# Value products and output projection laid into the heads of two attentions, with rotary keys padded to full height

## What is computed

```python
def mla_mixer(h, ...):
    proj = h @ w_in                                  # c_q 384, c_kv 256, k_pe 64
    q = rms_norm(c_q, q_a_norm) @ w_uq               # 8 heads x (128 + 64)
    kv = rms_norm(c_kv, kv_a_norm) @ w_ukv           # 8 heads x (128 keys + 128 values)
    q_pe, k_pe = rope(rms_norm(...)), rope(rms_norm(...))
    logits = (q_nope @ k_nope.T + q_pe @ k_pe.T) * scale     # causal
    return (softmax(logits) @ v) @ w_o

def moba_mixer(h, w_qkv, ...):                       # 256 tokens: one block, own keys only
    q, k, v = split(h @ w_qkv)
    logits = rms_norm(q) @ rms_norm(k).T * scale + rel_bias  # causal
    return (softmax(logits) @ v) @ w_o
```

## Time and profile before

| | us |
|---|---|
| median of 3 timed runs | 1106.78 |
| lowest and highest of them | 1105.79, 1111.33 |
| the profiled execution | 1100.91 |
| its span, first to last instruction | 1099.3 |
| TensorE busy | 1036.1 (94%) |
| VectorE busy | 703.4 (64%) |
| ScalarE busy | 529.1 (48%) |
| POOL busy | 99.2 (9%) |

### The profile page before, as it was taken

How to read it: one execution, slowest core, us unless ns; L and a number is a source line. 1 busy time by engine, 2 the same in 40 slices (tenths; PEclk the granted TensorE clock), 3 DMA queues, 4 the chain that set the end, 5 groups by cost and what they waited for, 6 DMA issues and landing times.

```text
span 1099.3 us, 15596 instructions
## 1 busy us (share of the span) xinstructions
PE 1036.1 (94%) x6112; PEld 886.9 (81%) x6112; DVE 703.4 (64%) x946; ACT 529.1 (48%) x712; POOL 99.2 (9%) x77
## 2 busy tenths in 40 slices
PE   7989899999999997989999999999999889999996
PEld 5556789888997875889999887988966678999995
DVE  5645556888736556557676754456477477777774
ACT  2463447766444557444554543553344255445442
POOL 0120004665000010000000000000000000000000
PEclk9997999999999999999999999999999999999998
DMA  8034466767643551547777542334100145445531
GB/s 351 1 126 104 153 232 251 274 241 272 255 158 115 191 191 44 219 159 269 280 281 283 198 184 78 115 118 151 39 1 1 43 175 200 176 172 186 200 148 57
DMA packets 29725, 183.89 MB, mean 167 GB/s; under 512 B 3440, under 2 KB 6128, under 8 KB 10096
## 3 DMA queue, kind: packets, MB, share of 16 engines
q1 hardware_dynamic: 25216, 156.84, 39.2%
q0 software_dynamic: 3456, 25.17, 6.5%
q10 hardware_dynamic: 1008, 1.27, 0.3%
HBM read 180.64 MB, written 2.62 MB: 167 GB/s over the span
## 4 chain that ended last, share of the span: by engine, by line
PE 74%; DVE 13%; ACT 6%; issue 3%; DMA 2%; POOL 1%; ACTq 0%; DVEq 0%; SPq 0%
PE bank L662 20%; PE bank L663 19%; PE bank L664 19%; DVE split L1795 4%; ACT split L1297 4%; PE bank L857 3%; PE bank L671 2%; DMA consts<-in_consts 2%; PE bank L1162 2%; PE bank L1143 1%; PE bank L945 1%; POOL stat L593 1%; PE bank L804 1%; DMA raw<-w_mlp 1%; ACT arena L1298 1%
## 5 line engine op out<-in xcount | busy, mean ns | idle before, releaser
L1795 DVE TENSOR_TENSOR split<-raw,split 128x2048 fp32r<-128x2048 f32 (+1 forms) x123 | 283.7, 2307 | 240.1 <-ACT split L1297 234.5
L1297 ACT ACTIVATE split<-raw 128x2048 fp32r<-128x2048 f32 (+1 forms) x123 | 233.6, 1899 | 267.7 <-PE bank L664 244.9
L662 PE MATMUL bank<-acts,split 128*128 128x256 f32 (+1 forms) x1024 | 290.6, 284 | 2.7 <-DVE acts L1833 1.4
L663 PE MATMUL bank<-acts,split 128*128 128x256 f32 (+1 forms) x1024 | 289.6, 283 | 0.0
L664 PE MATMUL bank<-acts,split 128*128 128x256 f32 (+1 forms) x1024 | 289.6, 283 | 0.0
L662 PE MATMUL bank<-split,acts 128*128 128x512 f32 (+1 forms) x544 | 214.4, 394 | 15.4 <-DVE split L1795 8.3
L663 PE MATMUL bank<-split,acts 128*128 128x512 f32 (+1 forms) x544 | 210.4, 387 | 0.0
L664 PE MATMUL bank<-split,acts 128*128 128x512 f32 (+1 forms) x544 | 210.3, 386 | 0.0
L662 PEld LDWEIGHTS bank<-acts,split 128*128 128x128 f32 (+1 forms) x1024 | 194.7, 190 | 6.2 <-issue 3.3
L663 PEld LDWEIGHTS bank<-acts,split 128*128 128x128 f32 (+1 forms) x1024 | 194.7, 190 | 2.3
L664 PEld LDWEIGHTS bank<-acts,split 128*128 128x128 f32 (+1 forms) x1024 | 194.7, 190 | 0.4
(11 more groups left out here) (245 smaller groups left out, 1189.6 us busy)
## 6 DMA issues: line engine op xcount, KB each, us to landing
raw<-w_mlp SPq DMA_DIRECT2D x64, 1024.0 KB, 4.9
raw<-w_glu SPq DMA_DIRECT2D x22, 1024.0 KB, 5.3
work<-w_ada POOLq DMA_DIRECT2D x12, 1024.0 KB, 5.1
raw<-w_qkv SPq DMA_DIRECT2D x12, 1024.0 KB, 4.8
bias<-w_ada POOLq DMA_DIRECT2D x12, 1024.0 KB, 5.1
arena<-w_glu_down SPq DMA_DIRECT2D x22, 512.0 KB, 3.3
raw<-w_mla_o SPq DMA_DIRECT2D x4, 1024.0 KB, 5.7
raw<-w_moba_o SPq DMA_DIRECT2D x4, 1024.0 KB, 4.8
```

Source lines behind the costliest of these rows:

```text
L662: pe.matmul(out_, a[0], b[0], start=first, stop=False)
L663: pe.matmul(out_, a[0], b[1], start=False, stop=False)
L1297: return act.activation(out_, in_, ACT.Copy)
L1795: v.tensor_tensor(split[:, c % 2, 1, 0:n], raw[:, c % 2, 0:n], split[:, c % 2, 0, 0:n].bitcast(F32), ALU.subtract).then_inc(lo_ready, 1)
```

## The change

1. **Rotary keys.** `kpT` becomes two tiles of full height: one holds the key in partitions 0 to 63 and zeros above, the other zeros below and the key in partitions 64 to 127. POOL writes the zeros after its third root. All four score matmuls of a head are now 128 partitions high.
2. **Value units, attention 0.** Of the four value units, unit 4 follows the rotary query transposes, unit 5 the key transposes, unit 6 stands after S2, unit 7 after O0. ScalarE empties them at matching places, the last two behind exponentials 0 and 1.
3. **Splits of mla_o.** The high part of chunk 0 is made by VectorE. The high part of chunk 1 is made by ScalarE in iteration 5 of the attention, its low part by VectorE in iteration 6; both came after the attention before.
4. **Value chunks, attention 1.** The loop covers only queries and keys, with a mean and a root for each. Queries are scaled and transposed first, then value chunks 0 and 1 are multiplied, keys transposed, then half of chunk 2; the other half stands after S2, the halves of chunk 3 after O0 and O1. The splits of chunks move with them.
5. **Projection.** Chunk 0 of either output projection is issued in two halves (by token tile), after O5 and after O6.
6. **Window attention.** Segment products of a step stand directly behind P(i).

```diff
@@ grid_order
         steps.append(("P", i))
+        steps.extend(x for x in SEGMENTS if SEGMENT_STEP.get(x) == i)
         if i + 3 < 2 * H:
             steps.append(("S", i + 3))
...
-        steps.extend(x for x in SEGMENTS if SEGMENT_STEP.get(x) == i)
@@ program
-        kpT = view(arena, 12288, T)
+        kpT = view(arena, 12288, T), view(arena, 12800, T)
@@ POOL
-            roots(0, 7)
+            roots(0, 3)
+            pool.wait_ge(roots_ready, 3)
+            pool.memset(kpT[0][64:128], 0.0).then_inc(kpe_zeros, 1)
+            pool.wait_ge(kpe_zeros, 1)
+            pool.memset(kpT[1][0:64], 0.0).then_inc(kpe_zeros, 1)
+            pool.wait_ge(kpe_zeros, 2)
+            roots(3, 7)
@@ TensorE
+            def out_products(name, g, t):
+                c, u = GC[name] + g, GU[name] + t
+                if t == 0:
+                    weights_in(c)
...
+            def first_out(name, attention, t):
+                for h in range(4):
+                    small_gone(pe, SU[attention] + unit_c[("O", h)])
+                out_products(name, 0, t)
...
+                    beside(kind, h)
...
-            ukv_products(1)
             pe.wait_ge(heads_normed, 3)
...
+            pe.wait_ge(front_w[7], 16)
+            ukv_products(1, 0)
             for n in range(4):
...
+            ukv_products(1, 1)
+            pe.wait_ge(kpe_zeros, 2)
             for u in range(SU["kpe"], SU["kn"] + 4):
                 small_gone(pe, u)
-            for u in range(4, 8):
-                gemm_gone(pe, GU["mla_ukv"] + u)
+            def beside0(kind, h):
+                if (kind, h) == ("S", 2):
+                    ukv_products(1, 2)
+                    for u in range(4, 6):
+                        gemm_gone(pe, GU["mla_ukv"] + u)
+                if (kind, h) == ("O", 0):
+                    ukv_products(1, 3)
+                if (kind, h) in (("O", 5), ("O", 6)):
+                    first_out("mla_o", "att0", h - 5)
...
             def scores0(u, h):
-                a = 64 * (h % 2)
...
-                pe.matmul(b[:, 0:T], qpT[a:a + 64, h // 2, P:T], kpT[a:a + 64, :], start=False, stop=True)
+                pe.matmul(b[:, 0:T], qpT[:, h // 2, P:T], kpT[h % 2][:, :], start=False, stop=True)
...
-            with pe.Fori(0, 3) as i:
+            with pe.Fori(0, 2) as i:
...
+            for n in range(4):
+                heads_flip(n)
+            for c in range(2):
+                for t in range(2):
+                    value_products(c, t)
+            pe.wait_ge(heads_normed, 7)
+            for n in range(4, 8):
+                heads_flip(n)
+            value_products(2, 0)
...
+            def beside1(kind, h):
+                if (kind, h) == ("S", 2):
+                    value_products(2, 1)
...
+                if (kind, h) in (("O", 0), ("O", 1)):
+                    value_products(3, h)
+                if (kind, h) in (("O", 5), ("O", 6)):
+                    first_out("moba_o", "att1", h - 5)
@@ ScalarE
-            for n in range(4, 8):
-                empty(GU["mla_ukv"] + n, kv[:, n % 2, 512 * (n // 2):512 * (n // 2) + 512])
-            split_hi(GC["mla_o"])
...
+            values_out(4)
             for n in range(4):
                 pair_empty(SU["kn"] + n, pair(knT, n), col("k_nope"))
+            values_out(5)
...
+            def beside0(h):
+                if h < 2:
+                    values_out(6 + h)
+                if h == 5:
+                    split_hi(GC["mla_o"] + 1)
...
+            used(c0 + 8)
+            used(c0 + 9)
+            values_out1(0)
+            values_out1(1)
             for n in range(4):
                 pair_empty(SU["k1"] + n, pair(k1T, n), col("moba_k"))
...
+            def beside1(h):
+                if h == 1:
+                    used(c0 + 10)
+                if h in (2, 3):
+                    values_out1(h)
+                if h == 5:
+                    used(c0 + 11)
@@ VectorE
+            v.wait_ge(w_loaded[0], 16)
+            v.tensor_copy(split[:, 0, 0, :], raw[:, 0, :]).then_inc(hi_ready, 1)
             split_lo(GC["mla_o"])
...
+            def beside0(h):
+                if h == 6:
+                    split_lo(GC["mla_o"] + 1)
...
+            def heads_scaled(n):
+                v.wait_ge(roots_ready, 10 + n)
...
+                    if (i, j) == (1, 1):
+                        heads_scaled(0)
+                v.wait_ge(sq_used, 14 + 4 * i)
+                means_of(8 + 16 * i, [(16, P)])
+            heads_scaled(1)
...
+            def beside1(h):
+                if h == 3:
+                    used(GC["qkv"] + 10)
+                if h == 6:
+                    used(GC["qkv"] + 11)

```

156 lines of the change are left out of this document (95 added, 61 removed).

## The result

The changed kernel takes **1076.7 us** (median of the first series, 1075.3 to 1081.7), the kernel before 1106.3 us (1102.7 to 1111.3): ratio 0.974, 95% interval 0.969 to 0.978. Of the four executions behind the 1106.3, three are those of the table of times before; the one that was new took 1102.7. Timed again in a second series, the changed kernel took 1078.3 us against 1103.2 for the kernel before: ratio 0.978 (0.977 to 0.980).

The account below looks back on a forecast made before the run. TensorE was taken as the bound: busy time, clock and idle time. Attention 0 (14.9), attention 1 (5.0) and window attention (1.5) save 21.4 us from 1100.91, giving 1079.5; adding 5.9 gives 1085.4 us, range 1079 to 1097.

Parts of the forecast that it names:

- carried-over offset: Whole kernel: the timed median lay 5.9 us above the profiled run, and this was added to the forecast.
- new waits: Attention 0: value copies and a split in ScalarE's queue delay outputs 0, 1 and 5, +2.6 us (0 to +5).
- the lead: Ahead of attention 0's scores: moved split and value units fill TensorE's idle time, -3.6 us.
- Attention 1: Second attention: reordered value and projection work cuts idle time and lets TensorE set the pace, -5.0 us (0 to -8).
- Window attention: Window attention loop: earlier segment products save half of TensorE's 2.9 us of waits, -1.5 us (-3 to +1).
- The clock term: Attention 0: with gap filled and tiles 128 high, full clock replaces 18.35 us at 0.54, -8.4 us.
- It fills nothing and is counted at 0: Output projection: moving its first chunk in halves behind outputs 5 and 6 only shifts its time, 0 us.
- Padding saves no time: Rival, score products: low tiles did not cause the 0.20 us steps, so 5.5 us are lost, 1090.9 us; chance 0.10.
- The clock falls anyway: Rival, attention 0: clock falls and stays low as long as before, +8.4 us, 1093.8 us; chance 0.11.
- ScalarE as the bound: Rival, attention 1: added copies and splits make ScalarE the limit, 5.0 us gone, 1090.4 us; chance 0.07.
- The low clock holds through attention 0: Rival, attention 0: low clock lasts up to the second projection chunk, 16 us slower than before, 1123 us; chance 0.04.
- Fillers that don't fill: Rival, both attentions' leads: idle time stays, 3.6 + 5.0 us lost, 1094.0 us; chance 0.04.

Follow-up runs that it names:

- pad_only: Kernel before with only the rotary keys padded, so every rotary score product is 128 high: 1095.0 us, ratio 0.991.
- no_pad: Changed kernel without the padding, rotary score products 64 high again, fillers kept: 1080.8 us, ratio 0.979.
- segments_only: Kernel before with only the window attention's segment product moved right behind the transposed probabilities: 1101.5 us, ratio 0.998.
- before_again: Kernel before, unchanged, timed and profiled again: 1103.6 us over 12 executions.
- out_inside: Kernel before with the first output projection chunk in halves behind outputs 5 and 6, attention 0's second-chunk split moved into the heads: 1102.6 us, ratio 0.998.
- spread_out: Changed kernel with the second-chunk split two heads later and the first projection chunk in four pieces between the last heads' steps: 1072.9 us.
- late_split: Changed kernel with the split of the second projection chunk two heads later in both attentions: 1076.2 us.
- out_behind: Changed kernel with the first chunk of both output projections back behind the last output: 1086.1 us.

## Why the prediction was wrong

The forecast misses the 1076.7 us of the first series by 8.7 us. For the account I take the second series (1103.2 and 1078.3), which has more executions and its own kernel before beside it: there the miss is 1085.4 - 1078.3 = 7.1 us, and two steps make up 6.7 of it; the rest is the clock's 0.1 and what medians leave over.

**The failed step is the carried-over offset.** "The median of the timed runs lies 5.9 us higher, at 1106.78; I carry this over" took three executions for the level of the kernel. Its medians over 9 to 23 executions are 1103.2 to 1105.1 in four series, and 1103.2 in this one: 3.6 us of the miss. An offset between a profiled execution and the others is nothing that a kernel keeps, as the step assumed: of the changed kernel the first profiled execution lay 5.0 us above its median (1081.7 and 1076.7), the second 8.2 below (1070.1 and 1078.3). The prediction also gave this step no width, although one profile and three times were 5 to 10 us apart. Without it the forecast would have been 1079.5 us. The first series' 1076.7 lies 1.6 us under the second's, which is within how far executions of one kernel differ.

**The second step that failed is the size of two terms at full clock**, that of attention 1 and above all that of the window attention; their mechanisms held. The terms at full clock were 3.6 + 5.5 - 2.6 + 5.0 + 1.5 = 13.0 us; 16.1 were measured (1080.4 - 1064.3, the executions of that series; the stages of the traces give 6.5 + 6.3 + 3.3 as well).
- Attention 0 without clock: 6.5 forecast, 48.6 - 42.1 = 6.5 measured. The exact hit is luck: 5.3 for the padding in pad_only (5.5 forecast), new waits 1.8 (2.6; 4.75 us ahead of outputs and chunk against 2.97 in the earlier trace rows), and 48.6 - 45.7 = 2.9 for the lead in no_pad, where all but 0.25 us of these waits are absent (3.6). The lead fell short by 0.7, the waits by 0.8, and the two cancel. The walk's own starts, 7.15 us less 3.44, also give 3.7 and not 3.6. And the 0.20 us and more "at every step" is misread: the four steps 0.53, 0.63, 0.42, 0.41 of the earlier trace rows are 0.43, 0.43, 0.23, 0.22 in pad_only, so the extra is 0.10 at the first and 0.19 to 0.20 at the others, 0.68 in all; the sum of 0.69 a head was right.
- Attention 1: 5.0 forecast; 10.0 + 1.5 - 5.7 = 5.8 by its rows, 5.5 to 6.3 by the stages, 4.6 when undone. The walk overstated the idle time left by 0.8 us, 6.5 for 5.7.
- Window attention: 1.5 forecast, 3.1 measured in segments_only (229.5 - 226.4), the mis-sized term. "I take half" had no row behind it.

**The clock term** was 8.4; 8.5 was measured as the difference of medians (20.9 - 12.4). The hole in attention 0 is worth its 8.5 us in the trace of before, 8.5 in before_again, 10.2 in segments_only and 15.4 in out_inside, and it is gone in every kernel without the gap. That far the mechanism was right. That the total came out to 0.1 us is luck: the rest of the clock did not stay as it was. Outside the hole the kernel before lost 18.7 - 8.5 = 10.2 us in its profile; the changed kernel lost 14.0 us in one profile, with new low stretches, one at 107 us among them, and 3.2 in the other. And the term rests on an edit that I counted at nothing. "It fills nothing and is counted at 0" holds at full clock (0.7 us) and fails for the clock: with the projection chunk behind the heads the same kernel loses 20.6 us to it instead of 12.4.

**The rivals.** Padding saves no time: refuted, though a third of it is eaten by waits that shorter heads expose. The clock falls anyway: refuted for attention 0. ScalarE as the bound: refuted. The low clock holds through attention 0: did not occur in the changed kernel, and did in out_inside, where the gap and the 64-high tiles were still there. Fillers that don't fill: refuted by 8.15 us busy of 8.30.

## What to carry to other kernels

When the granted clock varies between executions, compare span x clock and span x (1 - clock) apart: medians of the first repeated within 1 us over four series of one kernel and price edits of 2 us, the second tells whether an edit moved the clock. Take the level of a kernel from ten executions or more, and not from the profiled one and three others; even then it moved by 2 us between series, so compare with the kernel timed beside it. Lay independent full-rate work inside a gap rather than beside it (spread_out against late_split: 4.9 us at full clock for the same products in another order), and look which queue must deliver earlier once the gap is closed.

## What was not expected of the hardware

- What starts a low stretch and what keeps it seem to differ: with a gap of 2.3 us ahead of attention 0 one began there in all five profiles, without the gap in none of eight; 16.00 us of uninterrupted work with 64-high single-precision tiles in it did not end it (clock 0.50), and with the tiles padded to 128 it ended after 6.8 us (one profile).
- A change of tile height from one product to the next costs 0.1 to 0.2 us each time, because the load then starts with its product and not 0.21 us ahead of it; the loads of both heights are equally long there (0.29 and 0.30 us).
- Executions of one program on one chip differed by 8 and 12 us (1099.7 to 1107.3 before, 1070.1 to 1081.8 changed), while without the low time most agree within 1 us (53 of 70 before, all of these six): the same product at 107 us is followed by a fall in one execution and not in another.
- With its last heads 7.34 us busy of 9.50, out_behind had a fall in both attentions (0.64 and 0.51); with 5.45 us of dense products in the same heads the changed kernel had 1.00 there in both profiles (in one it fell right behind them).
